# Gated delta-rule recurrence: ScalarE's key sums, VectorE's gating and VectorE's sum of output squares move to other places in each head

## The reference, cut to what matters

```python
k = k * lax.rsqrt(jnp.sum(k * k, axis=-1, keepdims=True) + EPS)     # the key sums
diff = g_cum[..., :, None] - g_cum[..., None, :]                    # the differences
decay = jnp.where(causal, jnp.exp(jnp.where(causal, diff, 0.0)), 0.0)
L = jnp.where(strict, jnp.einsum('bhnid,bhnjd->bhnij', k_beta, k) * decay, 0.0)
T = lax.linalg.triangular_solve(eye + L, ...)
...
o = o * lax.rsqrt(jnp.mean(o * o, axis=-1, keepdims=True) + EPS) * w_onorm   # the output squares
return (o * jax.nn.silu(z)) @ w_out                                 # the gating
```

## Time and profile before

| what | value |
|---|---|
| median of 3 runs | 2017.26 us (2015.63 to 2017.3) |
| the profiled execution's own time | 2012.84 us |
| its span, first to last instruction | 2011.0 us |
| mean granted TensorE clock | 0.998 of full |
| busy: PE, DVE, ACT, POOL | 1969.1 us (98%), 1448.2 us (72%), 550.5 us (27%), 349.9 us (17%) |
| the GDN rounds with a recurrence in them | from about 530 to 880 us |

### The profile page before, as it was taken

The page is one execution under the profiler, slowest core; times in us unless marked ns, Lnnn a source line. Parts: engine busy times, 40 slices in busy tenths (PEclk is TensorE's granted clock), DMA queues, the critical chain, the costliest instruction groups (busy, mean ns, idle before and its releaser), DMA issues.

```text
span 2011.0 us, 31502 instructions
## 1 busy us (share of the span) xinstructions
PE 1969.1 (98%) x12790; PEld 1585.5 (79%) x12790; DVE 1448.2 (72%) x2209; ACT 550.5 (27%) x1063; POOL 349.9 (17%) x317
## 2 busy tenths in 40 slices
PE   9999999999999999999999999999999999999999
PEld 7888888887677777678888877777888888888887
DVE  6666766667876677768998887676666769859973
ACT  2000122222433333223884234574310010000000
POOL 2112111111101011012111212111121212222221
PEclk9999999999999999999999999999999999999999
DMA  5333322222211121222223322221233333333332
GB/s 182 96 93 105 91 83 90 91 89 65 75 59 60 56 67 49 65 61 87 64 64 95 117 94 87 70 64 53 74 93 96 105 95 97 102 95 95 95 100 89
DMA packets 52193, 171.26 MB, mean 85 GB/s; under 512 B 6329, under 2 KB 6585, under 8 KB 51921
## 3 DMA queue, kind: packets, MB, share of 16 engines
q1 hardware_dynamic: 48112, 161.33, 26.2%
q10 hardware_dynamic: 3936, 7.92, 1.3%
HBM read 167.07 MB, written 2.15 MB: 84 GB/s over the span
## 4 chain that ended last, share of the span: by engine, by line
PE 50%; DVE 7%; ACT 2%; issue 1%; DVEq 0%; ACTq 0%
PE ps_lin L1927 14%; PE ps_lin L1928 14%; PE ps_lin L1929 14%; PE ps_att L1976 3%; PE ps_aux L1976 2%; DVE arena L437 2%; DVE arena L431 2%; ACT arena L1347 1%; PE ps_att L1985 1%; DVE arena L434 1%; DVE w_lo L431 1%; PE ps_lin L1947 0%; DVE arena L982 0%; PE ps_lin L1948 0%; PE ps_lin L1949 0%
## 5 line engine op out<-in xcount | busy, mean ns | idle before, releaser
L1927 PE MATMUL ps_lin<-xw_hi,w_hi 128*128 128x512 f32 x1704 | 689.1, 404 | 2.0 <-DVE w_lo L431 1.9
L1929 PE MATMUL ps_lin<-xw_hi,w_lo 128*128 128x512 f32 x1704 | 665.7, 391 | 0.0
L1928 PE MATMUL ps_lin<-xw_lo,w_hi 128*128 128x512 f32 x1704 | 664.8, 390 | 0.0
L413 POOL TENSOR_SCALAR w_hi<-raw 128x1024 fp32r<-128x1024 f32 (+2 forms) x309 | 346.0, 1120 | 1641.9 <-PE ps_lin L1929 1515.3
L431 DVE TENSOR_TENSOR w_lo<-raw,w_hi 128x1024 fp32r<-128x1024 f32 (+2 forms) x340 | 379.3, 1118 | 45.7 <-POOL w_hi L413 17.5
L1347 ACT ACTIVATE arena<-arena 128x512 f32<-128x512 f32 (+9 forms) x336 | 196.0, 591 | 732.8 <-DVE arena L437 337.8
L1927 PEld LDWEIGHTS ps_lin<-xw_hi,w_hi 128*128 128x128 f32 x1704 | 320.6, 188 | 69.7 <-issue 3.5
L1929 PEld LDWEIGHTS ps_lin<-xw_hi,w_lo 128*128 128x128 f32 x1704 | 320.2, 188 | 68.8
L1928 PEld LDWEIGHTS ps_lin<-xw_lo,w_hi 128*128 128x128 f32 x1704 | 320.9, 188 | 58.8
L431 DVE TENSOR_TENSOR arena<-ps_lin,rstd 128x512 f32<-128x512 f32 (+3 forms) x220 | 147.7, 671 | 187.6 <-PE ps_lin L1929 179.2
L1927 PE MATMUL ps_lin<-y_hi,w_hi 128*128 128x512 f32 (+1 forms) x544 | 205.3, 377 | 0.0
(11 more groups left out here) (189 smaller groups left out, 1656.4 us busy)
## 6 DMA issues: line engine op xcount, KB each, us to landing
raw<-in_w_up SPq DMA_DIRECT2D x44, 512.0 KB, 3.6
raw<-in_conv_w_in SPq DMA_DIRECT2D x32, 512.0 KB, 3.6
raw<-in_fox_w_in SPq DMA_DIRECT2D x32, 512.0 KB, 3.6
raw<-in_gdn_w_in SPq DMA_DIRECT2D x32, 512.0 KB, 3.6
raw<-in_w_gate SPq DMA_DIRECT2D x24, 512.0 KB, 3.6
raw<-in_swa_w_in SPq DMA_DIRECT2D x20, 512.0 KB, 3.7
raw<-in_w_ml SPq DMA_DIRECT2D x16, 512.0 KB, 3.7
raw<-in_w_down SPq DMA_DIRECT2D x16, 512.0 KB, 3.6
```

Of the source, the lines that this page charges most:

```text
L413: pool.tensor_scalar(w_whole(n, kc * c)[0], w_raw(n, kc * c), 1.0, 0.0, mult, add).then_inc(s("w_rounded"), 1)
L1927: pe.matmul(o, wh, hi, start=first and k == 0, stop=False)
L1928: pe.matmul(o, wh, lo, start=False, stop=False)
L1929: ins = pe.matmul(o, wl, hi, start=False, stop=last and k == kc - 1)
```

## The change

Three steps of each head are issued at another place. No instruction is added or taken away, and TensorE's list stays as it was.

```diff
@@ VectorE, gdn_head @@
                 gdn_decay(h)
                 if h:
-                    gdn_out_squares(h - 1)
+                    gdn_gate(h - 1)
                 fill(GDN_FILL["tok"])
-                if h == GDN_H - 1:
-                    gdn_gate(h - 1)
                 dve.wait_ge(s("gdn_tok"), 2 * h + 1)
                 dve.wait_ge(s("gdn_kss"), h + 1)
...
                 dve.wait_ge(s("gdn_vb"), h + 1)
-                if 0 < h < GDN_H - 1:
-                    gdn_gate(h - 1)
...
                     fill(1)
+                if h < GDN_H - 1:
+                    gdn_out_squares(h)
@@ ScalarE @@
             def gdn_key_norms(h):
+                use(ACT.Exp)
                 act.wait_ge(s("gdn_tok"), 2 * h + 1)
...
             def gdn_head(h, fill):
+                gdn_key_norms(h)
                 gdn_decay(h)
-                gdn_key_norms(h)
                 fill(GDN_FILL["tok"])
```

## The result

| | before | changed |
|---|---|---|
| median of the runs, us | 2016.45 (2014.43 to 2017.3, 4 runs) | 1998.3 (1996.5 to 2000.91, 4 runs) |
| ratio, 95% interval | | 0.9912 (0.9895 to 0.993) |
| the profiled execution's own time, us | 2012.84 | 2000.91 |
| its span, us; mean granted clock | 2011.0; 0.998 | 1999.1; 0.997 |

The changed kernel is 0.9% faster. The forecast was 2001.3 with 1998.5 to 2006.0; against the baseline that it started from (2017.26), 15.9 us were forecast, 18 were measured in these runs and 15.3 and 15.7 in two later sets of runs. The profiled executions differ by only 11.9 us.

What follows compares the result with a forecast made beforehand. TensorE's holes, mainly waits for the gating and the sum of squares, were taken as the bound. Heads 1 to 6 (12.84), head 0 (2.3) and head 7 (0.8) give 15.9 us off 2017.26: 2001.3 us, range 1998.5 to 2006.

Steps and rivals of the forecast that it cites:

- The bound and the size of the holes: Heads 1 to 6: TensorE's waits for squares (0.65 us) and gating (1.49) cost 2.14 us a head, 12.84 in all.
- The bracketed 1.74: Heads 1 to 6: lower bound from bracketed idle times, 1.33 + 0.41 us a head, 10.4 us in all.
- The addition of squares: VectorE, heads 1 to 6: squares' hole gone with 2 us of slack; halves and differences 0.85 us later.
- The key sums: ScalarE, heads 1 to 6: they start at 749.10 instead of 752.18, so VectorE no longer waits its 1.59 us.
- What is late next: Heads 1 to 6, before level 1: evacuation 0.1 us late, transpose still ends 0.84 us before TensorE needs it.
- Head 0: Only the key sums matter: first product 2.31 us earlier, gain 2.3 us, or 1.8 by the skill's drain rule.
- Head 7: VectorE is slower here: only 0.8 us comes back, bounds 0 to 2.2, with some 3 us of new waits.
- a rival took its factor of 1.55: Heads 1 to 6: another wait takes a part through slowed VectorE operations, 6.5 us lost, 2007.8 us; chance 0.11.
- The clock rival: Head 7: the clock falls behind the moved hole, costing up to 1.7 us, 2003.0 us; chance 0.20.
- The sum: Whole kernel: 12.84 + 2.3 + 0.8 = 15.9 us; profiled execution about 1996.9, median 2001.3 us, chance 0.60.
- The two rivals in which heads 1 to 6 lose a part: Another wait takes a part, 2007.8 us, chance 0.11; A products still wait for `kd`, 2014.2 us, chance 0.05.
- The slower side: VectorE waits for ScalarE's late square with its list pushed behind: 2024.1 us if 4 us late; chance 0.04.

Runs made afterwards that it cites:

- both later edits: Changed kernel with round 0's w_lo halves one step earlier and head 7's w_lo subtraction moved to level 2: 1996.34 us, again 1996.36.
- p_all: Profile of the changed kernel with no further edit, run again beside its parts: median 2000.33 us, ratio 0.9923.

## Why the prediction was right

*The bound and the size of the holes.* Right. Against 2.14 us forecast, the three heads without an "issue" hole shrank by 2.22, 2.23 and 2.21 us; in head 5, A starts 2.13 us sooner after the key transposes. The bracketed 1.74 would have been too small. One reading is loose: "the same instructions without a wait" holds for A, but the 0.35 us behind the transposes is the distance to another product. The sum of squares came at 0.44, so its own hole was worth 0.56 us, and the product behind it came 0.65 sooner.

*The addition of squares.* Right that it costs nothing in the changed kernel, and VectorE's addition started 0.09 us behind the end of ScalarE's square where 0.1 was taken. The differences, counted from the key transposes, came 0.59 us later and not 0.85: the `w_lo` pair took 1.20 us from start to start instead of 1.44, since it no longer began beside POOL's rounding (which ended at 748.91 before, 741.04 after). The delay cost nothing only because ScalarE's order, changed too, had given this block room. The prediction didn't say that the part alone makes the kernel slower; the run did.

*The key sums.* Right, and worth more than the prediction's text suggests: alone they give 13.6 of the 15.3 us. The gating's move, which the prediction counts as a part of the 2.14, adds nothing to them that these runs can show.

*What is late next.* Right for heads 1 to 6. The slack before level 1 was computed as 0.84 us; in head 5 the transpose ended 0.91 us before TensorE asked.

*Head 0.* The term was mis-sized: 2.3 us forecast, 1.56 measured with the clock up. VectorE's chain did start 2.3 us earlier, but its decay product met POOL's rounding and took 0.74 us more. The step that failed is "Both hang on this chain, so the gain is the smaller of 2.31 and the holes", since it took the durations of the chain as fixed while its place against POOL moved. In the first profile there was no gain at all, because of the low clock ahead of it. No drain showed beside the ScalarE load: the load started 0.02 us behind the operation before it, and the first key sum 0.02 us behind the load's end (533.79 + 1.28, and 535.09). "ScalarE: Activation LUTs", What ACT_TABLE_LOAD costs, in the Trainium skill adds a drain to the load; the trace doesn't agree. The 1.56 us measured are nearer to the prediction's estimate by that page (1.8, which redone from the rows is 1.7) than to 2.3, but for another reason.

*Head 7.* The forecast of 0.8 us until the transpose was near: 0.97 us in the first profile, 1.25 and 1.53 in the two later ones of the same kernel. From there to the last addition the same three lost 1.3, 2.5 and 2.3 us, more than was gained. The new waits came in three places, and none for the transpose: 0.25 us for `kd`, 1.30 for a `w_lo` that the list of rows did not hold, and 0.64 for `spare`. The one for `w_lo` was missed. So is the reason for the 2.36 us of the two halves, from which a rival took its factor of 1.55: in the kernel before POOL rounds from 834.45 to 836.95 us there, and the halves end 0.54 us behind it. That is the same meeting as in head 0, so "nothing else is put beside these operations than before" was not a safe argument; moved operations can meet POOL. The clock rival was right in kind: the low clock stood behind the hole in level 2 in all three profiles of the changed kernel, and behind the moved wait for `w_lo` in two with both later edits.

*The sum.* 15.9 us forecast; 18.2, 15.3 and 15.7 measured between medians. That it came this near is partly luck. From profile to profile the spans differ by 11.9, 12.5 and 11.4 us only, and a profiled execution was forecast at 1996.9 us and took 2000.3 to 2001.4. In `p_all` against the kernel before, head 0 gave 1.5 us up to its transpose, heads 1 to 6 13.5, head 7 1.25; level 2 and what follows up to the last addition took back 2.5, and the rest of the program 1.3. The single profile of the kernel before, from which the sum starts, is faster than any other run of it, so the 4.4 us added for the median belonged to that one execution and not to profiling. The range is loose too: its ends by the terms named, with 1.7 us of spread, would be about 1998 and 2007, not 1998.5 and 2005. The two rivals in which heads 1 to 6 lose a part did not come up. The slower side did not either, in the changed kernel; its logic, VectorE's list pushed back as a block, is what the squares alone ran into.

## What to carry to other kernels

A wait that bears one engine's name may be removed by another engine's order: read back from the hole to the first idle time of the engine named, and ask what that one waited for. When an operation is moved ahead of a block, everything in the block is late by its length, so check each edit also without the others; one of the three here is a loss alone. And compute a hole from start to start against the same instructions elsewhere without a wait, not from modelled ends.

## What the runs showed of the hardware

A hole of TensorE can cost its length again. In 13 of the 14 profiles, between 520 and 900 us, a stretch at the lower of the two clock levels (1.2 GHz) began behind a hole of 1.3 to 2.7 us, and behind the same holes it stayed at 2.4 GHz in other executions; 4 us at 0.57 are 1.7 us of work. The time goes with it from run to run: of the changed kernel, the runs with a mean clock of 0.999 took 1996.5 and 1996.7 us, those with 0.997 took 1999.9 and 2000.9. It isn't all of the spread: runs of the kernel before with 0.997 go from 2014.5 to 2018.1 us. "TensorE: Matmul & The Clock Gate", What's actually happening, in the Trainium skill has idling throttle the clock; the traces agree, but not every hole of the same length did it: behind the one of 1.9 us before head 0, and behind the one in level 2 of head 7, it came in six of ten profiles each.

TensorE stopped after the same instruction, the 23rd of 64 small products, in ten of the eleven profiles with the subtraction in its old place, for 1.3 to 2.2 us and with nothing to wait for. The DMA rows of the changed kernel from 839.5 to 841.5 us hold no packet at all, and just before that, at 839.4, one packet of the queue for instructions had come behind the weight packets (queue, kind: packets, MB, share of the 16 engines, from 837.5 to 839.5 us):

```profile
q1 hardware_dynamic: 129, 0.46, 58.2%
q8 instruction: 1, 0.02, 2.7%
```

In all ten profiles such a packet stands in the last 0.8 us of the weight transfer or at its end, and TensorE goes on 2.2 to 2.5 us after it. In the eleventh, the key sums alone, it came at 838.3 us, with no weight packet between 838.0 and 839.0 (the same view, 838.0 to 839.0 us):

```profile
q8 instruction: 1, 0.02, 6.3%
```

The weight transfer began there only after 839.5, and TensorE has no long hole. In the three profiles with the transfer moved, the packet came alone as well (833.8, 835.3 and 833.0 us), and the long hole is gone. So the hole goes with an instruction packet that comes late, at the end of a weight transfer. That the packet is TensorE's code and had queued behind the weights is the reading that fits all of these; the packet's row doesn't say which engine it is for, so this stays an inference.
